# Output projection by column halves with the last tile's turn among the PLE products, and expert rows that start at another row group for each expert

## What is computed

```
a = RMSNorm(h);  z = a @ w_in                  # conv, attention and gate columns
merged = sum_r sigmoid(gate_r) * (y_r @ w_branch[r])
h += merged @ w_out                            # the output projection
m = RMSNorm(h)
logits = m @ w_router + b_router               # 32 experts, top 4 per row, softmax over the 4
h += sum_k gate_k * (swiglu(m @ w_up[e_k] + b_up[e_k]) @ w_down[e_k] + b_down[e_k])
h += sigmoid(RMSNorm(h) @ w_ple_gate) * (p @ w_ple)
y = RMSNorm(h)
```

## Time and profile before

| | us |
|---|---|
| median of 3 runs | 1505.54 |
| lowest, highest | 1504.8, 1507.93 |
| the profiled execution | 1509.31 |
| its span, first to last instruction | 1507.4 |
| TensorE busy (matmul) | 1464.5, 97% |
| VectorE busy | 733.7, 49% |
| ScalarE busy | 246.1, 16% |
| GpSimd busy | 96.8, 6% |
| HBM read, written | 478.54 MB, 29.79 MB |
| mean granted TensorE clock | 0.993 |

### The profile page before, as it was taken

The page is one execution under the profiler, slowest core; times in us unless marked ns, Lnnn a source line. Parts: engine busy times, 40 slices in busy tenths (PEclk is TensorE's granted clock), DMA queues, the critical chain, the costliest instruction groups (busy, mean ns, idle before and its releaser), DMA issues.

```text
span 1507.4 us, 37005 instructions
## 1 busy us (share of the span) xinstructions
PE 1464.5 (97%) x15688; PEld 813.7 (54%) x15688; DVE 733.7 (49%) x1633; ACT 246.1 (16%) x448; POOL 96.8 (6%) x130
## 2 busy tenths in 40 slices
...
DMA  8411922353999999999999999999999999999741
GB/s 281 146 66 48 322 85 85 132 207 141 398 407 405 411 412 402 412 411 414 414 406 408 412 412 413 412 403 412 414 414 412 410 402 411 412 411 384 308 157 47
DMA packets 83786, 492.16 MB, mean 326 GB/s; under 512 B 14135, under 2 KB 19495, under 8 KB 30356
## 3 DMA queue, kind: packets, MB, share of 16 engines
...
q10 hardware_dynamic: 96, 0.07, 0.0%
HBM read 478.54 MB, written 29.79 MB: 337 GB/s over the span
## 4 chain that ended last, share of the span: by engine, by line
PE 74%; DMA 14%; DVE 4%; SPq 4%; ACT 2%; issue 1%; DVEq 0%; POOLq 0%; ACTq 0%
PE ps L2445 32%; PE ps L2455 16%; PE ps L2040 10%; DMA raw<-w_up 9%; SPq L648 3%; PE ps L2231 3%; DMA raw<-w_down_rows 2%; DMA raw<-w_ple_chunks 2%; PE ps L1980 2%; PE ps L1982 2%; PE ps L1981 2%; PE ps L2424 1%; PE ps L2442 1%; ACT S L880 1%; DMA xg<-m_rows,iug 1%
## 5 line engine op out<-in xcount | busy, mean ns | idle before, releaser
L2445 PE MATMUL ps<-raw,xT 128*32 128x512 f32 x5688 | 620.3, 593 | 3.4 <-DMA raw<-w_up 3.3
L2445 PEld LDWEIGHTS ps<-raw,xT 128*32 128x32 f32 x5688 | 179.3, 110 | 428.5 <-issue 387.1
L2455 PE MATMUL ps<-raw,acT 128*32 128x256 f32 x5760 | 316.9, 379 | 3.2 <-DMA raw<-w_down_rows 3.2
L2455 PEld LDWEIGHTS ps<-raw,acT 128*32 128x32 f32 x5760 | 187.3, 110 | 139.6 <-issue 17.2
L1742 DVE TENSOR_SCALAR gl<-ps 128x256 f32<-128x256 f32 x94 | 34.2, 419 | 440.4 <-ACT gl L1062 440.4
L1784 DVE STREAM_TRANSPOSE acT<-arow 32x192 f32<-32x192 f32 (+1 forms) x512 | 187.1, 365 | 7.4
L1774 DVE STREAM_TRANSPOSE xT<-xg 32x256 f32<-32x256 f32 x372 | 161.8, 435 | 12.6 <-DMA xg<-m_rows,ius 6.9
L1062 ACT ACTIVATE gl<-ps 128x256 f32<-128x256 f32 x94 | 29.4, 384 | 650.5 <-PE ps L2445 623.3
L2040 PE MATMUL ps<-aTh,wh 128*128 128x272 f32 x512 | 107.3, 291 | 0.0
L2040 PE MATMUL ps<-aTh,wl 128*128 128x272 f32 x512 | 106.0, 288 | 0.0
L2040 PE MATMUL ps<-aTl,wh 128*128 128x272 f32 x512 | 105.6, 288 | 0.0
...
## 6 DMA issues: line engine op xcount, KB each, us to landing
raw<-w_up SPq DMA_DIRECT2D x253, 1024.0 KB
raw<-w_down_rows SPq DMA_DIRECT2D x128, 1024.0 KB, 26.0
raw<-w_mix SPq DMA_DIRECT2D x25, 1024.0 KB
...
yk<-y_rows SPq DMA_DIRECT2D x8, 1024.0 KB, 10.8
raw<-w_ple_chunks SPq DMA_DIRECT2D x4, 1024.0 KB, 7.8
ahead<-w_up SPq DMA_DIRECT2D x3, 1024.0 KB, 14.3
...
```

The source lines that it names most:

```text
L2445: ins = mmul(ps[32 * j:32 * j + 32, b, :], xT[:, k, 32 * g:32 * g + 32], w[:, 512 * q:512 * q + 512], start=False, stop=(k == UPC - 1))
L2455: ins = mmul(ps[32 * j:32 * j + 32, bank + b, 0:LB], a, raw[slot][:, D * (k % 2) + LB * q:D * (k % 2) + LB * q + LB], start=(k == 0), stop ...
```

## The change

w_out's chunks are put in the order column half, then row half (`mix`, WO_OF). `rows_half` does one column half of one tile in one PSUM bank: first halves of tiles 0 and 1 (interleaved), 2 and 3, with `p_turn` in tile 3; then the sample tile (`sample_out`); then the second halves of tiles 0 to 3. VectorE adds each half as it is done (`add_half`, `add_out`). Everything that follows a tile (statistics, turn, logits, route, stores, the running sum `before`) goes in ORDER = sample, 0, 1, 2, 3, and its semaphores count in that order (AT). The turn of the sample tile, its sums and its logits stand in the second half of tile 0; those of tile 0 in tile 1's, and so on. Tile 3's turn is in halves, one in its own second half, one among the PLE products, where its logits are too. The PLE products go 0, 4, 1, 2, 3, each step half a tile earlier against the tables. SP loads raw 5, 7, 10 and 11 when `sample_out` is done, raw 4 and 6 when the projection is done, raw 8 and 9 after the last store of m.

For the experts: `small_slots` gets six more instructions; expert e's slots begin 3*(e-1) further on (SPIN = 3), modulo 96, but not those of the small blocks in their first 64. The gathers and scatters of the small blocks move 64 rows instead of 96. The semaphores bd_half and ntr_half are folded into bd_mm and ntr, with the same points of waiting.

```diff
@@ -49,8 +49,8 @@
 SLOPE = [2.0 ** (-8.0 * (h + 1) / NH) for h in range(NH)]
 
 CH = 2048
-PP_ORDER = [4, 0, 1, 2, 3]
-PP_BANK = [1, 4, 1, 1, 4]
+PP_ORDER = [0, 4, 1, 2, 3]
+PP_BANK = [2, 1, 4, 1, 4]
 BIAS_SLOT = [3, 0, 3, 3, 3]
 GATE_SLOT = [1, 0, 1, 0, 1]
 RAW_MIX = 4
...
@@ -64,13 +64,16 @@
 BR_CHUNKS = 3 * PAIRS
 WO_CHUNKS = 4
 KH = KT // 2
-WO_OF = [[0, 1], [2, 3]]
+WO_OF = [[0, 2], [1, 3]]
+ORDER = [4, 0, 1, 2, 3]
+AT = [ORDER.index(i) for i in range(NT)]
 NM = Z_CHUNKS + BR_CHUNKS + WO_CHUNKS
 UPC, DNC = 8, 4
 BLK = UPC + DNC
 PEEL = 6
 SMALL = (2, 3)
 SCAP, SBANKS = 64, 2
+SPIN = 3
 STASH = 7
 MAXOVER = (T * TOPK - NEXP) // CAP
 NB = NEXP + MAXOVER
...
@@ -580,37 +583,40 @@
             sp.wait_ge(split_done, NM)
             sp.dma_start(raw[0][:], w_up[0, 0]).then_inc(landed[0], 16)
 
-            for i in range(NT):
-                if i == 1:
+            for n, i in enumerate(ORDER):
+                if n == 0:
                     sp.wait_ge(tr_done, NT + 1)
                     sp.dma_start(raw[2][:], w_up[0, 2]).then_inc(landed[2], 16)
-                if i == NT - 1:
+                    sp.wait_ge(tiles_done, TB - NT + 1)
+                    for m in (5, 7):
+                        sp.dma_start(raw[m][:], w_up[0, m]).then_inc(landed[m], 16)
+                    for m in (10, 11):
+                        sp.dma_start(raw[m][:], w_dn[0, m - UPC]).then_inc(landed[m], 16)
+                if n == NT - 1:
 
                     sp.wait_ge(tiles_done, TB)
                     sp.dma_start(iota[:], A["c_iota"]).then_inc(io_in, 16)
                     sp.dma_start(turn[:], A["c_turn"]).then_inc(io_in, 16)
                     sp.dma_start(bself[:], A["c_bsel"]).then_inc(io_in, 16)
-                    for m in (4, 5):
+                    for m in (4, 6):
                         sp.dma_start(raw[m][:], w_up[0, m]).then_inc(landed[m], 16)
                 rows = slice(P * i, P * i + ROWS[i])
-                sp.wait_ge(wo_ev, i + 1)
+                sp.wait_ge(wo_ev, n + 1)
                 if i < NT - 1:
                     sp.dma_start(h_dram[rows], hrow[:, i, :]).then_inc(h_out, 16)
                 else:
                     for j in range(4):
                         sp.dma_start(h_dram[rows, QD * j:QD * j + QD], hrow[TS * j:TS * j + TS, i, 0:QD]).then_inc(h_out, 16)
-                sp.wait_ge(m_done, i + 1)
+                sp.wait_ge(m_done, n + 1)
                 if i < NT - 1:
-                    sp.dma_start(m_dram[rows], mrow[:, i % 2, :]).then_inc(rows_out[i % 2], 16)
+                    sp.dma_start(m_dram[rows], mrow[:, n % 2, :]).then_inc(rows_out[n % 2], 16)
                 else:
                     for j in range(4):
-                        sp.dma_start(m_dram[rows, QD * j:QD * j + QD], mrow[TS * j:TS * j + TS, i % 2, 0:QD]).then_inc(rows_out[0], 16)
+                        sp.dma_start(m_dram[rows, QD * j:QD * j + QD], mrow[TS * j:TS * j + TS, n % 2, 0:QD]).then_inc(rows_out[0], 16)
             sp.wait_ge(b_out, 32)
             for j in range(2):
                 sp.dma_start(bup[4 * j:4 * j + 4].bitcast(F32), bs_dram[0, j, 0:2 * FF].rearrange("(q n) -> q n", n=512)).then_inc(bup_in, 16)
-            for m in (6, 7):
-                sp.dma_start(raw[m][:], w_up[0, m]).then_inc(landed[m], 16)
-            for c in range(DNC):
+            for c in (0, 1):
                 sp.dma_start(raw[UPC + c][:], w_dn[0, c]).then_inc(landed[UPC + c], 16)
             sp.wait_ge(pp_mm, NT)
             sp.dma_start(raw[3][:], w_up[0, 3]).then_inc(landed[3], 16)
...
@@ -738,9 +744,9 @@
                 pool.drain()
                 rows_from(iug[0:CAP, 0:1])
 
-            def rows_to(index):
-
-                nc.gpsimd.indirect_dma_start(y_dram, bass.IndirectOffsetOnAxis(ap=index, axis=0), yrow[0:CAP], None,
...
                     pool.wait_ge(y_side, b - 2)
-                    rows_to(dsti[0:CAP, b - 3:b - 2])
+                    count = SCAP if b - 3 in SMALL else CAP
+                    rows_to(dsti[0:count, b - 3:b - 2], count)
             with pool.Fori(PEEL, last) as i:
 
                 pool.wait_ge(xh_done, i + 1)
...
-                    act.wait_ge(ple_in, 16)
-                    nc.scalar.activation(pl_h[:], raw[3][:], ACT.Copy).then_inc(pl_hi, 1)
-            act.wait_ge(folded, 1)
-            nc.scalar.activation(std[:, 4:5], ps[:, 0, 300:301], ACT.Sqrt, scale=1.0 / D, bias=epsb[:, 0:1]).then_inc(std_done, 1)
+                else:
+                    act.wait_ge(folded, 1)
+                    nc.scalar.activation(std[:, 4:5], ps[:, 5, 0:1], ACT.Sqrt, scale=1.0 / D, bias=epsb[:, 0:1]).then_inc(std_done, 1)
 
             def pp_copy(n):
 
...
 
+            def add_half(i):
+
+                dve.wait_ge(out_half, i + 1)
+                nc.vector.tensor_tensor(hrow[:, i, 0:512], ps[:, i, :], hrow[:, i, 0:512], ALU.add).then_inc(half_added, 1)
+
             def add_out(i):
 
-                w = WF[i]
-                dve.wait_ge(tiles_done, TB - NT + i + 1)
-                nc.vector.tensor_tensor(hrow[:, i, 0:w], slot2(i % 2)[:, 0:w], hrow[:, i, 0:w], ALU.add).then_inc(wo_ev, 1)
+                n = AT[i]
+                dve.wait_ge(tiles_done, TB - NT + n + 1)
+                if i < NT - 1:
+                    nc.vector.tensor_tensor(hrow[:, i, 512:D], ps[:, n % 4, :], hrow[:, i, 512:D], ALU.add).then_inc(wo_ev, 1)
+                else:
+                    nc.vector.tensor_tensor(hrow[:, i, 0:QD], ps[:, 0, 0:QD], hrow[:, i, 0:QD], ALU.add).then_inc(wo_ev, 1)
...
+                    nc.vector.tensor_tensor(before[:, ORDER[n + 1], :], before[:, i, :], mask[:, i, :], ALU.add).then_inc(r_step, 1)
                 else:
                     nc.vector.tensor_tensor(all4[:], before[:, i, :].unsqueeze(1).broadcast_to([P, 4, NEXP]),
                                             mask[:, i, :].unsqueeze(1).broadcast_to([P, 4, NEXP]), ALU.add).then_inc(r_step, 1)
 
-            for i in range(NT):
-                if i < NT - 1:
-                    if i != 1:
-                        add_out(i)
-                    m_rows(i)
-                if i == 0:
-                    p_low()
-                    add_out(1)
-                if i == NT - 2:
-                    add_out(i + 1)
-                if i == NT - 1:
-                    m_rows(i)
+            add_half(0)
+            add_half(1)
+            add_half(2)
+            p_low()
+            add_half(3)
+            dve.wait_ge(pl_hi, 1)
+            nc.vector.tensor_tensor(pl_l[:], raw[3][:], pl_h[:].bitcast(F32), ALU.subtract).then_inc(pl_lo, 1)
+            add_out(ORDER[0])
+            for n, i in enumerate(ORDER):
+                m_rows(i)
+                if n + 1 < NT:
+                    add_out(ORDER[n + 1])
                 route(i)
-                if i == 1:
-                    dve.wait_ge(pl_hi, 1)
-                    nc.vector.tensor_tensor(pl_l[:], raw[3][:], pl_h[:].bitcast(F32), ALU.subtract).then_inc(pl_lo, 1)
             b = R0S + ROUT * NT
 
...
@@ -1677,6 +1703,16 @@
                 nc.vector.scalar_tensor_tensor(out=moved[:], in0=turned[:], scalar=float(1 - 16 * each), in1=moved[:], op0=ALU.mult,
                                                op1=ALU.add).then_inc(order_step, 1)
                 dve.wait_ge(order_step, 19)
+                nc.vector.tensor_scalar(flag0[:], flag0[:], -float(SPIN), float(SPIN), ALU.mult, ALU.add).then_inc(order_step, 1)
+                nc.vector.tensor_scalar(turned[:], topf[:].rearrange("p i k -> p (i k)"), -1.0, 0.0, ALU.add, ALU.max).then_inc(order_step, 1)
+                dve.wait_ge(order_step, 21)
+                nc.vector.tensor_tensor(turned[:], turned[:], flag0[:], ALU.mult).then_inc(order_step, 1)
+                nc.vector.tensor_tensor(slot[:], slot[:], moved[:], ALU.add).then_inc(order_step, 1)
+                dve.wait_ge(order_step, 23)
+                nc.vector.tensor_tensor(slot[:], slot[:], turned[:], ALU.add).then_inc(order_step, 1)
+                dve.wait_ge(order_step, 24)
+                nc.vector.tensor_scalar(moved[:], slot[:], float(CAP), -float(CAP), ALU.is_ge, ALU.mult).then_inc(order_step, 1)
+                dve.wait_ge(order_step, 25)
                 nc.vector.tensor_tensor(slot[:], slot[:], moved[:], ALU.add).then_inc(r_step, 1)
 
             def slot_entries():
...
-                            seen = k + 1
+            def rows_half(i, ch, bank, steps=range(KT), between=()):
+
+                tok = slice(P * i, P * i + P)
+                for k in steps:
+                    g = 2 * ch + k // KH
+                    if i == 0 and ch == 0:
+                        pe.wait_ge(mg_l, k + 1)
                         if k % KH == 0:
                             pe.wait_ge(split_done, Z_CHUNKS + BR_CHUNKS + g + 1)
                     w_h = wo_h[g][:].rearrange("p (k n) -> p k n", k=KH)
                     w_l = wo_l[g][:].rearrange("p (k n) -> p k n", k=KH)
```

(74 more changed lines are left out.)

191 lines of the change are left out of this document (92 added, 99 removed).

## The result

The changed kernel takes 1497.78 us (median of five runs, 1496.5 to 1499.12); the kernel before takes 1506.5 in five runs on the same chip (1504.8 to 1507.93). The ratio is 0.9942 with a 95% interval of 0.993 to 0.9954, a gain of 8.7 us, between 6.9 and 10.5. The forecast was 10 us less, 1495.5 against the median known then. The profiled execution of after took 1498.28 us, its span is 1496.4 us; against that of before the span is 11.0 us shorter, 2.3 us more than the medians say.

The account below looks back on a forecast made before the run. Loads set the end, with TensorE having at most 9.5 us of waits to give. Loads ahead 3.5 + turned groups 6.8 = 10.3, taken as 10: 1505.54 - 10 = 1495.5 us; range 1490.5 to 1502, widened by half a microsecond.

Parts of the forecast that it names:

- The bound: Expert blocks: the loads set the end, and TensorE has at most 9.5 us of waits to give.
- Groups turned, 6.8 us: Expert gathers and scatters: fullest row group falls from 158 to 140 rows, landings 6.8 us earlier by the last block.
- The run-out that I took as proof: DMA from 1400 us: nine of 16 row groups stay on, 0.56, against a share of 0.54 from 1402 us.
- Loads ahead, 3.5 us: Before block 0: four chunks load from about 338 us, putting the stream 3.5 us ahead; bounds 0 and 10.2.
- The projection, 1.7 us: Projection in column halves: block 0 begins 1.7 us earlier; bounds 4 us later, 3 us earlier.
- The last gather: Before block 0: m's store lands at about 378 us, the gather at 384 us; 387.9 if it takes 9.43 us.
- The tail, "the same 10 us: no more, no less": After the last block: the gate chunk, and the products with yh behind it, move by the same 10 us.
- A: Rival, expert blocks: another engine (7) is the slow one; the change gains 1.7 to 4.3, about 1502; chance 0.14.
- B: Rival, expert blocks: engine 15 is slow, landings 3.8 us later; 1509.3, or 1505.8 with the loads ahead; chance 0.07.
- C: Rival, tail: the stream gains more, the 3.9 us wait for yh goes too; 15 us, 1490.5; chance 0.13.
- D: Rival, projection: it doesn't do what it says, or a missed wait and the late gather; under 3 us; chance 0.06.
- The signs: Small-block waits under 1 us, landings 25 us or less at 1130, chunks near 338, steep DMA fall after about 1405.

Follow-up runs that it names:

- where the growth is 3.5 us: The changed kernel with the eight bias rows of a block in one transfer instead of two of four: 1498.2 us, ratio 0.994 to the kernel before.
- without both parts: The changed kernel without the turned groups and with all gathers and scatters of 96 rows: 1504.4 us, ratio 0.9982 to the kernel before.
- start at 1: Every expert from the third on begins one slot further on, not 3*(e-1): 1503.0 us in the changed kernel, 1507.5 us in the kernel before.
- start at 4: Every expert from the third on begins four slots further on, not 3*(e-1): 1497.7 us in the changed kernel, 1503.7 us in the kernel before.
- late loads: The changed kernel with the four early loads put back behind the store of the last tile: 1504.9 us, ratio 0.9992 to the kernel before.
- the turned kernel: The kernel before with the turned row groups alone (SPIN = 3); projection, loads and transfer sizes as they were: 1502.3 us, ratio 0.9971.
- start at 8: The kernel before with every expert from the third on started at the same eighth slot: 1501.4 us, ratio 0.9962.

## Why the prediction was right, and where it wasn't

*The bound.* Right: the loads set the end. That TensorE had 9.5 us of waits to give was read from the list, which leaves out the short ones: it gave 9.3 us between block 0 and the products with yh and still has 4.6 us of listed waits, where I had 0.5 early and almost none late. 1.7 to 3.3 us of them stay in the last block of every kernel, also where the growth is 3.5 us. The 10 us of the forecast lie within the interval of the gain, 6.9 to 10.5.

*Groups turned, 6.8 us.* The size was right (6.3 us), the reason only half. The step that failed is "if each DMA engine serves six consecutive rows, the groups get 158 ..." taken as the whole load of an engine. The map held; the bias rows on groups 0 to 3 were left out, worth 14 rows or more where the fullest group is 22 above the mean. SPIN works because it takes the extra rows off those four groups, 158 to 137, not because it evens all 16. That the size came out all the same is partly luck: with all starts at 0 the fullest groups are groups 0 to 3, and with the turned ones groups 0 to 3 (137) and the fullest (140) are nearly level, so the two rules ask for nearly the same. The run-out that I took as proof, 0.54 for nine of 16 groups, fits both, and the window behind it, shown above, has 0.68, which fits neither count. Its tail didn't fit: 0.31 at 1410 us is five engines, four with bias rows nearly fit, and I had noted "about five" without asking which.

*Loads ahead, 3.5 us.* Sized against the kernel before, with the projection, it came out: 2.7 us for both. As a term of its own it was mis-sized: without them the changed kernel is 7.1 us slower. I had priced the stream but not what the later queue does to the last gather. Inside the term two steps were off. The four chunks are issued from 340.8 us on, about as said, but the engines have work until 387 us (I had the chunks ahead of the gather done by 381.4), and raw 3 comes hardly earlier: 80.7 us after the first product of the projection in after (390.43 - 309.73) and 80.8 before (387.98 - 307.16), where I had 1.7 us. The engines stand idle just ahead of it, with a share of 0.25 at 388 to 389 us and 0.00 from there to 391.

*The projection, 1.7 us.* Counted from its first product (307.16 us before, 309.73 in after), block 0 begins after 83.45 us before and after 82.33 us in after; it is 82.33 without both parts and 82.32 with the start at 1 and at 4. That is 1.1 us earlier, inside the bounds and less than said. The profiled run of after begins it later by the clock of the span, at 392.06 us against 390.61:

```profile
390.24 0.82 PE L2520 MATMUL ps<-ident,xg 96*128 96x96 f32 x8
...
392.06 0.93 PE L2479 MATMUL ps<-bup,bsel 8*128 8x512 f32 x3
```

That run came to its projection 2.6 us later than that of before. 1.5 us of it are two waits before 60 us (for qTl and kvT), which the profile of the changed kernel with the start at 4 has too and the others don't; that kernel begins its projection at 308.60 us, four others with the new projection between 306.92 and 307.90. Where the rest of the 2.6 us comes from is not shown. There is no wait of TensorE from 300 us to block 0, so the new waits cost nothing, as costed.

*The last gather.* Wrong in both halves, with no effect on the time. I had m land at 378 us; its store took 8.9 us behind raw 4, raw 6 and h, and the gather could only be issued at 384.35 us:

```profile
384.35 1.18 POOL L738 DMA_INDIRECT xg<-m_rows,iug  x1 [352.79 <-DMA m_rows<-mrow]
```

Then it took 5.2 us, not 9.43, as the loads ahead of it came to their end: the DMA share was 1.04 at 386 to 387 us, 0.85 and 0.25 in the next two, then 0.00. It landed at 389.6 us for a use at 390.24. This and the 8.6 us of the late loads agree with a gather that is slow only while something is queued. The margin is under 1 us, and the experiment shows the price beyond it.

*The tail, "the same 10 us: no more, no less".* The products with yh moved from 1418.68 to 1410.84 us, 7.8 us. The other 3.2 us of the span come after it, and they are not the change's. In the profiled run of before, an add of two took 3.45 us (its like take 1.2; the profile of the turned kernel has such a one too, behind a split of the gate chunk that is 1.9 us shorter there), TensorE waited 4.48 us for xnb, and the granted clock fell again:

```profile
1446.36 1.69 PE L2595 MATMUL ps<-ident,xnb 128*128 128x128 f32 x8 [4.48 <-DVE xnb L1898]
```

```profile
1442.00:1446.00 4.00, 0.00 (x0) 0.00 (x0) 3.93 (x3) 1.15 (x2) 3.22 (x1) 1.00 0.50 140
1446.00:1450.00 4.00, 3.65 (x14) 3.17 (x15) 1.24 (x3) 1.21 (x2) 0.00 (x0) 0.59 1.03 419
```

The same place of after:

```profile
1436.33 1.09 PE L2631 MATMUL ps<-ident,xnb 128*128 128x128 f32 x8 [2.27 <-DVE xnb L1934]
```

From the products with yh to the end of the span it is 88.7 us in that run, 85.6 in after, and 85.3 (turned alone) and 84.5 (start at 8) in two kernels with the old tail code. So the forecast for the tail holds with 8 us in the place of 10.

*Rivals.* A and B (engines 7 or 15 slow by themselves) are out as the ones that set the end: group 7 with 152 rows instead of 142 (start at 4) and group 15 with 121 to 129 instead of 116 (starts at 4, at 8 and turned) went with a gain. C didn't come: TensorE still waits 3.8 us for yh, as the last gate chunk is there only at 1408.31 us. D came true in one kernel of the experiments, the one with the late loads.

*The signs.* The waits around the small blocks are under 1 us each (0.8 the longest), the four chunks go out near 341 us, and there is no gap on TensorE between 338 us and block 0. The landing at 1130 us is 25.6 us, just over the 25, and the steep fall of all engines from 1405 us on didn't come: the share is 0.82 from 1402 us on and 0.76 at 1406 to 1408.
